# One decoder layer on one core: the expert down matrices of the first pass move from SyncE's DMA queue to GpSimd's

## What is computed

```python
for e in range(N_EXPERTS):                       # 32
    a = xt @ w_gate_up[e] + b_gate_up[e]         # (T, 1024) @ (1024, 2048)
    gate = jnp.minimum(a[:, :D_FF], SWIGLU_LIMIT)
    up = jnp.clip(a[:, D_FF:], -SWIGLU_LIMIT, SWIGLU_LIMIT)
    h = (up + 1.0) * gate * jax.nn.sigmoid(SWIGLU_ALPHA * gate)
    out = out + combine[:, e:e + 1] * (h @ w_down[e] + b_down[e])   # (T, 1024) @ (1024, 1024)
```

## Time and profile before

| | |
|---|---|
| median of three runs | 1382.72 us |
| profiled execution | 1383.47 us |
| its span in the trace | 1381.7 us |
| TensorE busy | 1320.4 us (96%) |
| weight load of TensorE | 706.5 us (51%) |
| VectorE, ScalarE, GpSimd busy | 351.2, 265.9, 90.9 us |
| SyncE's DMA queue (q1) | 453.39 MB |
| GpSimd's DMA queue (q0) | 44.50 MB |
| gate and up pieces, issue to landing | 29.1 us (median) |
| down pieces, issue to landing | 22.5 us (median) |

### The profile page before, as it was taken

How to read it: one execution, slowest core, us unless ns; L and a number is a source line. 1 busy time by engine, 2 the same in 40 slices (tenths; PEclk the granted TensorE clock), 3 DMA queues, 4 the chain that set the end, 5 groups by cost and what they waited for, 6 DMA issues and landing times.

```text
span 1381.7 us, 17763 instructions
## 1 busy us (share of the span) xinstructions
PE 1320.4 (96%) x7269; PEld 706.5 (51%) x7269; DVE 351.2 (25%) x765; ACT 265.9 (19%) x577; POOL 90.9 (7%) x117
## 2 busy tenths in 40 slices
PE   9999999999999999999998989989999998998987
PEld 7757886788887443443342433424344243342433
DVE  4844333210245421221220212212122021220212
ACT  4325344321134310110111101101011010111102
POOL 1641212100200000000000000000000000000000
PEclk9999999999999999999999999999999999999999
DMA  9792657628938999999999999999999999999996
GB/s 337 277 342 94 212 206 271 227 92 298 361 133 328 349 409 430 427 428 429 428 429 429 428 428 429 428 417 411 431 429 427 429 429 428 430 427 430 426 429 258
DMA packets 64197, 499.08 MB, mean 361 GB/s; under 512 B 5535, under 2 KB 6760, under 8 KB 39192
## 3 DMA queue, kind: packets, MB, share of 16 engines
q1 hardware_dynamic: 51192, 453.39, 79.4%
q0 software_dynamic: 12800, 44.50, 9.0%
q10 hardware_dynamic: 160, 0.56, 0.1%
HBM read 491.34 MB, written 7.08 MB: 361 GB/s over the span
## 4 chain that ended last, share of the span: by engine, by line
PE 77%; DMA 19%; DVE 2%; issue 1%; ACT 1%; SPq 0%; POOL 0%; DVEq 0%
PE bank L1279 21%; PE bank L754 17%; PE bank L1299 13%; DMA arena<-in_w_down 10%; DMA ring<-in_w_gate_up 9%; PE bank L1333 4%; PE bank L1263 4%; PE bank L713 3%; PE bank L726 2%; PE bank L1288 1%; PE bank L788 1%; PE bank L1216 1%; PE bank L1130 1%; PE bank L1294 1%; PE bank L880 1%
## 5 line engine op out<-in xcount | busy, mean ns | idle before, releaser
L1279 PE MATMUL bank<-ring,arena 128*64 128x512 f32 x1536 | 344.8, 597 | 5.9 <-DMA ring<-in_w_gate_up 5.9
L1299 PE MATMUL bank<-arena 128*64 128x512 f32 x1000 | 230.7, 613 | 31.4 <-DMA arena<-in_w_down 31.4
L754 PE MATMUL bank<-arena,ring 128*128 128x264 f32 x1024 | 235.5, 388 | 3.2 <-ACT arena L1490 1.8
L1279 PEld LDWEIGHTS bank<-ring,arena 128*64 128x64 f32 x1536 | 104.1, 137 | 222.0 <-issue 207.0
L754 PEld LDWEIGHTS bank<-arena,ring 128*128 128x128 f32 x1024 | 191.8, 190 | 39.6 <-issue 6.4
L1299 PEld LDWEIGHTS bank<-arena 128*64 128x64 f32 x1000 | 71.0, 140 | 176.8 <-issue 131.3
L2437 DVE TENSOR_TENSOR resid<-resid,bank 128x264 f32<-128x264 f32 x128 | 55.0, 429 | 358.8 <-PE bank L1333 357.3
L1279 PE MATMUL bank<-arena 128*64 128x512 f32 x512 | 115.5, 593 | 3.1 <-DMA arena<-in_w_gate_up 3.1
L2442 DVE TENSOR_SCALAR arena<-bank 128x512 f32<-128x512 f32 x32 | 22.0, 688 | 349.4 <-PE bank L1279 349.4
L1861 ACT COPY arena<-bank 64x512 f32<-64x512 f32 x63 | 36.5, 580 | 234.4 <-PE bank L1299 233.6
L1490 ACT ACTIVATE arena<-bank 128x264 f32<-128x264 f32 (+5 forms) x128 | 50.2, 402 | 163.3 <-PE bank L754 135.7
(11 more groups left out here) (329 smaller groups left out, 945.8 us busy)
## 6 DMA issues: line engine op xcount, KB each, us to landing
ring<-in_w_gate_up SPq DMA_DIRECT2D x95, 2048.0 KB, 29.1
arena<-in_w_down SPq DMA_DIRECT2D x62, 2048.0 KB, 22.5
arena<-in_w_gate_up SPq DMA_DIRECT2D x32, 2048.0 KB, 28.7
ring<-in_w_in SPq DMA_DIRECT2D x10, 2048.0 KB, 10.2
out<-arena POOLq DMA_DIRECT2D x8, 512.0 KB, 4.6
ring<-v_rows POOLq DMA_DIRECT2D x8, 512.0 KB, 5.8
ring<-in_w_o_mla SPq DMA_DIRECT2D x2, 2048.0 KB, 9.5
ring<-in_w_o_gla SPq DMA_DIRECT2D x2, 2048.0 KB, 16.5
```

Of the source, the lines that this page charges most:

```text
L754: mm = nc.tensor.matmul(lin_bank(name)[0:m, 0:width], w(ring_name, nk, cols)[:, k, a:a + m], rhs[:, k, 0:width], start=(k == 0), stop=(k = ...
L1279: mm = nc.tensor.matmul(B[i // 2][CAP * (i % 2):CAP * (i % 2) + CAP, :], xg[:, k, CAP * e:CAP * e + CAP], slot(n)[:, a:a + 512], start=Fal ...
L1299: mm = nc.tensor.matmul(B[4][CAP * half:CAP * half + CAP, :], hT[:, k % 4, CAP * (k // 4):CAP * (k // 4) + CAP], weights[:, 512 * half:512 ...
```

## The change

The first pass gets a list of its own on SyncE, `gate_up_loads_of_first_pass`, with the gate and up pieces alone and, at its end, the four pieces of the last down matrix. GpSimd issues the down pieces of experts 0 to 30 behind its earlier transfers: the first half of expert 0's as soon as `xs` is there, ahead of the transfers of the biases; the second half behind the waits for `lg`, for six transposes of rows and for the states, which SyncE had before; and then a loop of 30 rounds, in each of which it waits for slot 8, issues, waits for slot 9, issues. The list for a second pass is as it was, except that its first lines no longer serve the first pass. What TensorE, VectorE and ScalarE do is unchanged.

```diff
+            def gate_up_loads_of_first_pass():
...
+                load_gate_up(2, 0, 1, 1, 4)
+                load_gate_up(3, 1, 1)
+                with sp.Fori(1, NE // 2 - 1) as q:
+                    load_gate_up(2 * q + 2, 0, q + 1)
+                    load_gate_up(2 * q + 3, 1, q + 1)
+                load_last_down(0)
...
             load_expert(6, gate_up_of(0, 3))
-            load_expert(DOWN_SLOT[0], down_of(0, 0))
...
             load_expert(0, gate_up_of(1, 2))
-            lin_full(sp, "lg")
-            sp.wait_ge(S("rows_turned"), 6)
-            state_out(sp, 0)
-            state_out(sp, 1)
-            load_expert(DOWN_SLOT[1], down_of(0, 1))
-            loads_of_pass(0)
+            gate_up_loads_of_first_pass()
...
             memory_values(0, 5)
+            def load_down_half(e, h):
...
+                n = DOWN_SLOT[h]
+                pool.dma_start(slot(n).rearrange("p (c n) -> p c n", n=D), rows).then_inc(S(f"slot{n}_loaded"), 16)
+
+            lin_full(pool, "xs")
+            load_down_half(0, 0)
             lin_full(pool, "xpv0")
...
             for i in range(NST):
                 state_out(pool, i)
+            lin_full(pool, "lg")
+            pool.wait_ge(S("rows_turned"), 6)
+            load_down_half(0, 1)
+            with pool.Fori(1, NE - 1) as e:
+                for h in range(2):
+                    pool.wait_ge(S(f"slot{DOWN_SLOT[h]}_used"), e)
+                    load_down_half(e, h)
```

More of the change, by code:

```diff
@@ L488, in load_down, with load_last_down @@
                     load_expert(DOWN_SLOT[h], down_of(e, h), used)
-            def loads_of_pass(p):
[L492 to L500, removed]
+            def load_last_down(p):
+                for i, n in enumerate(LAST_DOWN_SLOT):
+                    sp.wait_ge(S(f"slot{n}_used"), p * (NE // 2 + 1) + NE // 2)
+                    sp.dma_start(slot(n)[:, 0:2 * D].rearrange("p (c n) -> p c n", n=D), down_of(NE - 1, i // 2)[:, 2 * (i % 2):2 * (i % 2) + 2, :])\
+                        .then_inc(S(f"slot{n}_loaded"), 16)
+            def gate_up_loads_of_first_pass():
+                first_half, second_half = (slot(3)[:, 2 * DFF * c:2 * DFF * c + 2 * DFF][:, None, :] for c in range(2))
+                sp.wait_ge(S("first_row_used"), 1)
+                sp.dma_start(first_half, gate_up_of(2, 0)[:, 0:1, :]).then_inc(S("slot3_loaded"), 16)
+                sp.wait_ge(S("slot3_used"), 1)
+                sp.dma_start(second_half, gate_up_of(2, 0)[:, 1:2, :]).then_inc(S("slot3_loaded"), 16)
+                load_gate_up(2, 0, 1, 1, 4)
[4 more added lines that the diff above has]
+                load_last_down(0)
+            def loads_of_pass(p):
+                load_gate_up(2, 0, p * (NE // 2 + 1) + 1)
                 load_gate_up(3, 1, p * (NE // 2) + 1)
@@ L522, in loads_of_pass @@
                 load_expert(DOWN_SLOT[1], down_of(NE - 2, 1), p * N_DOWN + NE - 2)
[L523 to L526, removed]
+                load_last_down(p)
             last_reader = {RING_SLOT[n]: reader for n, (_, reader) in enumerate(RING)}
@@ L686, in _ @@
             memory_values(0, 5)
+            def load_down_half(e, h):
+                if isinstance(e, int):
+                    rows = w_down[0, e].rearrange("(h p c) n -> p h c n", p=P, h=2)[:, h]
+                else:
+                    rows = w_down[0, bass.ds(e, 1)].rearrange("o (h p c) n -> p (o h) c n", p=P, h=2)[:, h]
+                n = DOWN_SLOT[h]
+                pool.dma_start(slot(n).rearrange("p (c n) -> p c n", n=D), rows).then_inc(S(f"slot{n}_loaded"), 16)
+            lin_full(pool, "xs")
+            load_down_half(0, 0)
             lin_full(pool, "xpv0")
```

## The result

The changed kernel takes 1395.88 us (median of four runs, 1395.02 to 1396.71), the kernel before, run beside it, 1382.73 us. The ratio on record is 1.0086, with a 95% interval of 1.0073 to 1.0100; the two medians alone would give 1.0095. The forecast was 1388.5 us: the direction was right, the loss was 2.3 times the 5.8 us forecast. The profiled execution took 1395.17 us, its span is 1393.4 us, 11.7 us more than before.

What follows compares the result with a forecast made beforehand. The prediction took the kernel as bound by bytes from about 670 us on; -2.2 (dent) + 0.5 (start) + 7.5 (end) = +5.8 us gave a median of 1388.5 us, range 1380.5 to 1400.

Steps and rivals of the forecast that it cites:

- What bounds the kernel: Experts from about 670 us: bound by bytes at 428.6 GB/s, TensorE having 5.7 us to spare in each pair.
- The dent: DMA rate from 925 to 975 us, where SyncE's list changes order: a separate gate and up list gains 2.2 us.
- The start: Around 508 us, down slots reloaded by GpSimd, whose transfers start late beside other traffic: +0.5 us, bounds 0 and +4.
- The two queues: SyncE's and GpSimd's queues: same total rate, alternating packet by packet, half each (214 GB/s) while both have work.
- Rivals 3 and 4: GpSimd's queue costs more per byte, 1390 to 1425 us (chance 0.11); two queues move more, 1370 to 1380 us (0.13).
- The end: Last experts: TensorE ends 10.5 us after the last byte, where before it was 3.0; a loss of 7.5 us.
- It waits for the odd expert's fourth piece in each pair: TensorE in each expert pair: wants that gate and up piece at 53.06 us, but it lands at 58.5.
- Rival 1: Last experts: the end costs nothing, as gate pieces land earlier; 1380.5 to 1385.4 us, chance 0.25.
- Rival 2: Last experts: down pieces come too late, at a share below about 0.45 of the rate; 1392 to 1398 us, chance 0.13.

Runs made afterwards that it cites:

- e3: The changed kernel with GpSimd loading the down pieces of experts 0 to 14 alone, the old list from expert 15 on; ratio 1.0044 to the kernel before.
- e5: The kernel before, with SyncE's list keeping its first part's order (down pieces ahead of the fourth gate and up piece) up to expert 27; ratio 1.0052.
- e9: The kernel before, with the change of order in SyncE's list made in steps over experts 16 to 23; ratio 0.9991.
- change_again: The changed kernel run once more, unaltered, as yardstick on another chip; ratio 1.0061 to the kernel before.
- e11: The changed kernel with TensorE's pair 14 written out of its loop; ratio 1.0091 with useless matmuls (fillers) ahead of the last two waits, 1.0078 without.
- e8: The changed kernel with GpSimd's down pieces each cut in two transfers, with rows of 8 KB a partition instead of 16; ratio 1.0272 to the kernel before.
- e4: The kernel before, with only the down matrices of experts 27 to 30 on GpSimd's queue; ratio 1.0073.
- e6: The changed kernel with 8 and 5 useless matmuls in each pair, all into one half of a bank; ratio 1.0821 to the kernel before.

## Why the prediction was off

**What bounds the kernel: right.** Bytes at 428 GB/s, with the end set by TensorE's work behind them. The strip and the equal last landing show it.

**The dent, -2.2 us: right.** Gone in the changed kernel. e3, e5 and e9 show that it comes from the place where a list changes its order.

**The start, +0.5 us: small, right in sign.** From 500 to 520 us 377 GB/s were moved, against 397 before: 2.4 us lost instead of 1.4, so +1.0. Another 1.0 us is the run's own: the whole of its time axis is about 1 us late from the first 12 us on (a matmul group starts at 11.61 instead of 10.56, the gate and up piece of the earlier trace rows is issued at 425.58 instead of 424.51), ahead of anything that was changed. -2.2 + 1.0 + 1.0 gives the last landing that was measured.

**The two queues: right.** DMA queues of the changed kernel from 1312 to 1316, 1316 to 1320 and 1320 to 1324 us, with the issue of down 29's first half by GpSimd (last row):

```profile
q1 hardware_dynamic: 118, 1.70, 100.1%
...
q0 software_dynamic: 59, 0.97, 56.5%
q1 hardware_dynamic: 48, 0.75, 44.4%
...
q0 software_dynamic: 53, 0.87, 50.8%
q1 hardware_dynamic: 54, 0.82, 48.3%
```

```profile
1312.30 0.53 POOL L696 DMA_DIRECT2D arena<-in_w_down  x1 [33.37 <-PE bank L1319]
```

Both terms of it, packet by packet and 4 us late, came true. Rivals 3 and 4 are out: 174.5 MB on q0, and 428 GB/s, neither less nor more. The Trainium skill ("DMA: Bandwidth & Descriptors", Rules for kernel authors) says that spreading DMAs over engines doesn't help bandwidth, as they interleave on the same 16 engines; the 428 of both strips agree. The Trainium skill ("DMA: Bandwidth & Descriptors", Latency and other measured facts) says that engines 7 and 15 are usually slower, by its guess through GpSimd's descriptor rings. With 130 MB more on GpSimd's queue the level didn't move, so no cost of that kind shows here; the engines weren't read one by one.

**The end, +7.5 us: this is the step that failed.** It was measured at about 12 us (15.0 less 3.0), 4.5 us more than forecast, out of the 5.9 us by which the profiled loss of 11.7 exceeds the forecast of 5.8. Its parts can be read one by one. With t = 0 at the start of expert 29's fourth piece (1297.50):

- Transfers left: forecast 68.5 us, measured 1366.15 - 1297.50 = 68.65. Right.
- Down 29 issued: forecast t = 12.6, measured 14.8 (1312.30). Of the 2.2 us, 1.5 are the group of t = 0 at a low clock, 5.08 us instead of 3.60. I had counted the wait and not what stands behind it.
- From that issue to the start of down 29's second half: forecast 24.2 us, measured 24.93 (change_again 24.76, e11 25.1 and 25.3).
- From there to the end: forecast 42.2 us, measured 43.94, again the clock, 5.35 us instead of 3.65.

14.8 + 24.9 + 43.9 = 83.7, where I had 79.0; 83.7 - 68.65 = 15.0 is the measured gap. So the mechanism was the forecast's, and the step that failed is its sum of TensorE's work after t = 0: 79.0 us forecast, 83.7 measured. The mis-sized terms are two slow groups, which the forecast put at nothing, 3.2 us in this trace, and 1.4 us of issue and landing. The clock term is read from rows; only its second half, 1.7 us, was seen to go in an experiment. change_again shows that its parts vary: 3.0 us behind the first wait and nothing behind the last. That the two sums agree within 0.2 us may be chance. The remaining 1.5 us between a loss of 13.2 us in the medians and of 11.7 us in the profiles is the spread of single executions.

**"It waits for the odd expert's fourth piece in each pair": wrong, though the end didn't need it.** From 520 us on the changed kernel does so in five pairs only, four of them:

```profile
885.14 3.65 PE L1299 MATMUL bank<-arena 128*64 128x512 f32 x16 [2.02 <-DMA arena<-in_w_gate_up]
...
945.10 5.35 PE L1299 MATMUL bank<-arena 128*64 128x512 f32 x16 [4.47 <-DMA arena<-in_w_gate_up]
...
1062.58 6.49 PE L1299 MATMUL bank<-arena 128*64 128x512 f32 x16 [4.92 <-DMA arena<-in_w_gate_up]
...
1180.04 5.35 PE L1299 MATMUL bank<-arena 128*64 128x512 f32 x16 [3.74 <-DMA arena<-in_w_gate_up]
```

From 520 to 1280 us the odd expert's down product waits for 1.9 to 2.5 us in each pair; a pair takes 55 us then, faster than its bytes, until the stock is used up and one pair pays with a wait of 4 to 5 us. Which pair pays depends on small shifts: in e11 without fillers it wasn't the last one, and the end was the same within 1.2 us.

**The rivals.** Rival 1 was out by the gap of 15.0 us. Rival 2's time (1392 to 1398) holds the result, but its condition, a share below 0.45, doesn't: the shares were equal. e8 made that condition, and it cost far more. A time that fits says nothing for a cause that is refuted. Its sign was an end over 15 us behind the last landing; at the measured 15.0 the gap alone doesn't decide, and the shares do.

## What to carry to other kernels

When a stage is bound by bytes and the DMA engines stay busy, a list that is blocked costs nothing, as the 769 us of waits on SyncE did here. What counts is that pieces land in the order in which they are used, and that at the last large wait enough bytes are still under way to cover the work behind it. To move transfers that are needed soon onto a second queue takes this order out of your hands: here the queues alternated packet by packet, and each took half of the rate, whichever piece was needed first. Before such a change, count for the last stages how much work is left at the last byte, and put a lower clock into the groups that follow a wait of some us.

## What the runs showed of the hardware

- Two DMA queues at work shared the engines by packets, and a packet was here one partition's row: 53 to 54 packets with rows of 16 KB on both, 88 to 86 with 8 KB against 16 KB, and then 0.59 MB to 1.16.
- A queue that joined a busy one had no packet for about 4 us, GpSimd's (issued 1312.30, none before 1316) and ScalarE's hardware queue (issued 1332.60, none before 1336) alike. The forecast took it for a trait of GpSimd's.
- TensorE's granted clock was 0.67 to 0.70 over the group behind waits of 3.0 and 4.9 us, a loss of 1.5 to 1.7 us each, and 0.54 to 0.55 behind two other waits of 4.92 us (changed kernel at 1062.58, 6.49 us; change_again at 1303.05, 6.56 us), a loss of 2.9 to 3.0 us; behind waits of 2 to 3 us it was seen both fallen (changed kernel at 808.05, 2.04 us: 5.35 us; e4, 2.74 us: 5.35 us) and not (change_again, 2.82 us: 3.65 us).
- Matmuls of 64 columns in float32 that alternate between the halves of a bank took 0.22 us for each record of the profile (4.46 us for 20, e11), those into the same half 0.44 (6.60 us for 15, e6), both without a wait and at full clock.
